# Two-layer decoder step on one core: the adaLN modulation computed tile by tile, most of it between other work

## What is computed

```python
for l in range(DEPTH):
    mod = (jax.nn.silu(c) @ p['w_ada'][l] + p['b_ada'][l])[:, None, :]
    shift1, scale1, gate1, shift2, scale2, gate2 = jnp.split(mod, 6, axis=-1)
    h = rmsnorm(x, p['g_mix'][l]) * (1 + scale1) + shift1
    mix, nb_a, nb_c, nb_d, v_n = token_mixers(h, buf_a[l], buf_c[l], buf_d[l], start_pos, l, p)
    x = x + gate1 * mix
    h = rmsnorm(x, p['g_ffn'][l]) * (1 + scale2) + shift2
    ...
    x = x + gate2 * f
```

## Time and profile before

| | |
|---|---|
| time, 3 runs | 1733.95, 1734.02, 1735.37 us (median 1734.02) |
| the profiled execution | 1732.69 us, its span from the first to the last instruction 1730.9 us |
| mean granted TensorE clock | 0.941 of full speed |
| busy: PE / PEld / DVE / ACT / POOL | 1488.1 / 1425.0 / 600.9 / 461.0 / 398.0 us |
| modulation's matmuls (L791), 768 | 104.0 us busy |
| modulation's rests on DVE (L1403), 48 | 110.0 us busy, 2293 ns each |
| modulation's rounding on ACT (L1157), 48 | 91.7 us busy, 1911 ns each |
| loads of `w_ada`, 48 of 1,024 KB | 11.2 us from issue to landing |

### The profile page before, as it was taken

The page is one execution under the profiler, slowest core; times in us unless marked ns, Lnnn a source line. Parts: engine busy times, 40 slices in busy tenths (PEclk is TensorE's granted clock), DMA queues, the critical chain, the costliest instruction groups (busy, mean ns, idle before and its releaser), DMA issues.

```text
span 1730.9 us, 26002 instructions
## 1 busy us (share of the span) xinstructions
PE 1488.1 (86%) x11320; PEld 1425.0 (82%) x11320; DVE 600.9 (35%) x815; ACT 461.0 (27%) x646; POOL 398.0 (23%) x288
## 2 busy tenths in 40 slices
PE   5777794797999999998968784999999986999992
PEld 4555694697999999997957682999999986999992
DVE  6757598734102111014696622011110110010115
ACT  6767421433222122222313312111111110010114
POOL 1101571253344333443450512000000000000005
PEclk9999897899999999998988897999999997999995
DMA  9999231113423323233221027589789792658644
GB/s 319 326 308 348 67 98 32 41 59 118 126 74 100 108 74 98 58 101 98 74 73 49 6 71 271 193 272 334 242 286 318 271 309 76 216 164 300 228 146 169
DMA packets 249973, 286.70 MB, mean 166 GB/s; under 512 B 7469, under 2 KB 241599, under 8 KB 249814
## 3 DMA queue, kind: packets, MB, share of 16 engines
q1 hardware_dynamic: 244886, 272.17, 48.4%
q0 software_dynamic: 3760, 12.09, 1.9%
q10 hardware_dynamic: 1200, 0.56, 0.1%
HBM read 266.45 MB, written 19.07 MB: 165 GB/s over the span
## 4 chain that ended last, share of the span: by engine, by line
PE 71%; DVE 15%; DMA 5%; issue 4%; SPq 2%; ACT 2%; POOL 1%; POOLq 0%; DVEq 0%; ACTq 0%
PE PP L746 29%; PE PP L1014 21%; PE PP L1026 11%; DVE work L1499 7%; DMA mem<-in_w_ada 4%; PE PP L759 2%; PE PP L791 2%; DVE stat L1595 2%; PE PP L720 1%; PE PP L731 1%; PE PP L985 1%; PE PP L996 1%; DVE stat L1428 1%; DVE mem L1441 1%; DVE mem_r L1437 1%
## 5 line engine op out<-in xcount | busy, mean ns | idle before, releaser
L746 PE MATMUL PP<-hT_r,mem_r 128*128 128x260 f32 x2624 | 428.5, 284 | 4.6 <-DVE xT L1453 3.2
L1014 PE MATMUL PP<-big,mem 128*128 128x144 f32 (+2 forms) x2816 | 372.9, 295 | 22.8 <-issue 22.0
L1014 PEld LDWEIGHTS PP<-big,mem 128*128 128x128 f32 x2816 | 370.7, 191 | 23.5 <-issue 22.4
L604 POOL TENSOR_TENSOR mem_r<-mem,mem_r 128x1024 fp32r<-128x1024 f32 (+1 forms) x108 | 279.0, 2598 | 407.7 <-ACT mem_r L1141 407.0
L746 PEld LDWEIGHTS PP<-hT_r,mem_r 128*128 128x128 f32 x2624 | 362.5, 189 | 6.5 <-issue 2.5
L746 PE MATMUL PP<-mem_r 128*128 128x260 f32 x1312 | 263.8, 283 | 0.0
L746 PEld LDWEIGHTS PP<-mem_r 128*128 128x128 f32 x1312 | 201.7, 188 | 0.0
L1026 PE MATMUL PP<-big,mem 128*128 128x144 f32 (+2 forms) x1408 | 193.5, 294 | 0.0
L1026 PEld LDWEIGHTS PP<-big,mem 128*128 128x128 f32 x1408 | 186.6, 190 | 0.0
L1689 DVE TENSOR_TENSOR big<-PP,stat 128x256 f32<-128x256 f32 x88 | 37.4, 425 | 394.4 <-ACT stat L1324 394.4
L702 POOL DMA_INDIRECT mem<-y_by_expert,place x10 | 9.9, 986 | 624.5 <-SPq L534 621.8
(11 more groups left out here) (236 smaller groups left out, 1100.5 us busy)
## 6 DMA issues: line engine op xcount, KB each, us to landing
mem<-in_w_moe SPq DMA_DIRECT2D x48, 1536.0 KB, 8.8
mem<-in_w_ada SPq DMA_DIRECT2D x48, 1024.0 KB, 11.2
mem<-in_w_moe SPq DMA_DIRECT2D x32, 1408.0 KB, 9.4
mem<-in_w_dense SPq DMA_DIRECT2D x20, 1024.0 KB, 5.5
mem<-in_w_in SPq DMA_DIRECT2D x16, 1024.0 KB, 5.4
mem<-in_w_moe SPq DMA_DIRECT2D x16, 1024.0 KB, 6.8
mem<-in_w_dense SPq DMA_DIRECT2D x16, 704.0 KB, 4.7
mem<-in_w_out SPq DMA_DIRECT2D x8, 1024.0 KB, 5.1
```

Source lines behind the costliest of these rows:

```text
L604: pool.tensor_tensor(r_(raw), raw, read_(hi), ALU.subtract).then_inc(w_lo, 1)
L746: mm = pe.matmul(PP[q][:, h, 0:HT], r_(w[:, k, :]), r_(x[:, k, HT * h:HT * h + HT]), start=(i == 0 and w is wh and x is hi), stop=(i == le ...
L1014: mm = pe.matmul(PP[w][:, f % 2, 0:n], raw[:, w, k, :], hn[:, k, 0:n], start=(k == 0), stop=(k == KD - 1))
```

## The change

The modulation of the first norm (16 tiles: shift1 and scale1 of layer 0) is computed up front in four pairs of chunks (`first_pair`), the other 80 tiles (`ADA`) later, in fills (`ada_fill`) at the places of `ADA_AT`. A tile is now a plain fp32 product with the weights stationary (128 x 128) and `c` moving: 9 columns, 8 matmuls a tile, straight into channel-major form. The rounding on ACT, the rests on DVE, the turning by transposes and POOL's part fall away; DVE adds the bias from PSUM (`mod_out`).

- Layer 0's mixer: 3 tiles after each of q = 4 to 11 (24). Layer 1's: 3 after each of q = 3 to 11 (27).
- Second norm of layer 0 and first norm of layer 1: 5 each, between the norm's sums and `two_products`.
- Dense part: 3 after each even f of the first half (18), 1 after f = 0 of the second.

Their weights come in tiles of 512 KB (rows of 128 channels, 512 bytes) into a ring of three in `adaw`; SP issues a tile's load when the tile three before it is done (`ada_loads`), queued between the other weights' loads. The results wait in the spare columns of PP3's second bank. SP now loads the tokens first, then pair 0, the small vectors, pair 1, the mixer's inputs; pairs 2 and 3 (pair 2 lies in `work`, the place of the squares) after the norm's sums.

```diff
-ADA_RING = 6
-NA = 24 // ADA_RING
+ADA_RING = 3
...
+ADA = [(0, j) for j in range(16, 48)] + [(1, j) for j in range(48)]
+IN_FILLS = [[(q, 3) for q in range(4, 12)], [(q, 3) for q in range(3, 12)]]
+FF_FILLS = [(0, f, 3) for f in range(0, 12, 2)] + [(1, 0, 1)]
+NORM_FILL = 5
+ADA_AT = {}
+_at = 0
+for _key, _n in ([(("in", 0, q), n) for q, n in IN_FILLS[0]] + [(("norm", 1), NORM_FILL)]
+                 + [(("ff", h, f), n) for h, f, n in FF_FILLS] + [(("norm", 2), NORM_FILL)]
+                 + [(("in", 1, q), n) for q, n in IN_FILLS[1]]):
+    ADA_AT[_key] = (_at, _at + _n)
+    _at += _n
+PAIRS_OUT = 4
+GROUPS = [("in", 0), ("norm", 1)] + [("ff", h, f) for h, f, _ in FF_FILLS] + [("norm", 2), ("in", 1)]
...
+        first_ada = [cut(mem, RING * SLOT, KD, 256), cut(mem, (RING + 1) * SLOT, KD, 256),
+                     cut(big, 5 * D + 4 * P + D, KD, 256), cut(big, 5 * D + 4 * P + D + SLOT, KD, 256),
+                     cut(wflat, 0, KD, 256), cut(wflat, SLOT, KD, 256),
+                     cut(mem, 2 * SLOT, KD, 256), cut(mem, 3 * SLOT, KD, 256)]
...
-            def ada_load(j, l, b):
-                sp.dma_start(ada_slot(j), w_ada_v[l][b]).then_inc(efull[j], 16)
+            def ada_loads(first, last):
+
+                for g in range(first, min(last, len(ADA))):
+                    l, j = ADA[g]
+                    if g >= ADA_RING:
+                        sp.wait_ge(ada_mm, 16 + g - ADA_RING + 1)
+                    sp.dma_start(adaw[:, g % ADA_RING], w_ada_v[l][j // 2][:, :, P * (j % 2):P * (j % 2) + P]).then_inc(ada_full[g % ADA_RING], 16)
+
+            def ada_after(*key):
+
+                first, last = ADA_AT[key]
+                ada_loads(first + ADA_RING, last + ADA_RING)
...
+            def first_pair(i):
+
+                for c, b in enumerate((4 + i, i)):
+                    sp.dma_start(first_ada[2 * i + c], w_ada_v[0][b]).then_inc(ada_in[i], 16)
...
+            for t in range(4):
+                sp.dma_start(xin[:, t, :], A["x_prompt"][0, P * t:P * t + P, :]).then_inc(x_in, 16)
+            sp.dma_start(xin[0:NS, 4, :], A["x_sample"].rearrange("b s d -> (b s) d")).then_inc(x_in, 16)
...
+            first_pair(0)
...
+            first_pair(1)
+            load(WIN0, chunk(WIN0))
+            mixer_loads(0)
+            sp.wait_ge(*norm_step(0, "sum", 1))
+            first_pair(2)
+            load(WIN0 + 1, chunk(WIN0 + 1))
+            first_pair(3)
+            ada_loads(0, ADA_RING)
+            for j in (2, 3):
+                sp.wait_ge(ada_mm, 12 + 2 * j - 2)
+                load(WIN0 + j, chunk(WIN0 + j))
             for n in range(WIN0, MOE - RING):
+                for l, base in ((0, WIN0), (1, WIN1)):
...
+            def ada_fill(*key):
+
+                for g in range(*ADA_AT[key]):
+                    first = min(a for k, (a, _) in ADA_AT.items() if k == key or (key[0] == "in" and k[:2] == key[:2]))
+                    at = HT + NQ * (g - first)
+                    pe.wait_ge(ada_full[g % ADA_RING], 16 * (g // ADA_RING + 1))
+                    for k in range(KD):
+                        mm = pe.matmul(PP[3][:, 1, at:at + NQ], adaw[:, g % ADA_RING, k, :], cs[:, k, :], start=(k == 0), stop=(k == KD - 1))
+                    mm.then_inc(ada_mm, 1)
+
+            def first_pair(i):
+
+                pe.wait_ge(ada_in[i], 32)
+                if i >= 2:
+                    pe.wait_ge(ada_out, i - 1)
+                for c in range(2):
+                    for m in range(2):
+                        at = NQ * (2 * c + m)
                         for k in range(KD):
-                            for lower, w in enumerate((ahi[:, j % 3], ada_slot(j))):
-                                mm = pe.matmul(PP[0][0:2 * NQ, j % 2, 0:256], r_(cs[:, k, :]), r_(w[:, k, :]),
-                                               start=(k == 0 and not lower), stop=(k == KD - 1 and bool(lower)))
+                            mm = pe.matmul(PP[1][:, i % 2, at:at + NQ], first_ada[2 * i + c][:, k, P * m:P * m + P], cs[:, k, :],
+                                           start=(k == 0), stop=(k == KD - 1))
                         mm.then_inc(ada_mm, 1)
-                        if j % 3 == 2:
-                            pe.wait_ge(ada_row, n + 3)
-                            for m in range(2):
-                                tr = pe.transpose(PP[1][:, 0, m * P:(m + 1) * P], modrow[:, m * P:(m + 1) * P], ident[:])
-                            tr.then_inc(ada_tr, 1)
...
+            first_pair(0)
+            pe.wait_ge(vec_in, 16 * NVEC)
+            for v in range(DEPTH):
+                tr = pe.transpose(PP[3][:, 0, v * NROWS:(v + 1) * NROWS], rows[0:NROWS, v, :], ident[0:NROWS, 0:NROWS])
+            tr.then_inc(pro_tr, 1)
+            pe.wait_ge(pro_dve, 8)
+            pe.wait_ge(const_dve, 1)
+            for j in range(KD):
+                norm_sum(0, j)
+            mixer_start(0)
+            for i in range(1, 4):
+                first_pair(i)
...
+                    pe.wait_ge(*ada_out_after("ff", 1, 0))
+                    ada_fill("norm", 2)
...
+                    if ("in", l, q) in ADA_AT:
+                        if l and q == 3:
+                            pe.wait_ge(*ada_out_after("norm", 2))
+                        ada_fill("in", l, q)
...
+                            if ("ff", h, f) in ADA_AT:
+                                if h == f == 0:
+                                    pe.wait_ge(*ada_out_after("norm", 1))
+                                if f:
+                                    pe.wait_ge(ff_free, FH * h + f)
+                                ada_fill("ff", h, f)
...
-                        dve.wait_ge(ada_hi, 24 * l + ADA_RING * i + j + 1)
-                        dve.tensor_tensor(r_(ada_slot(j)), ada_slot(j), read_(ahi[:, j % 3]), ALU.subtract).then_inc(ada_lo, 1)
...
+            def first_pair(i):
+
+                dve.wait_ge(ada_mm, 4 * i + 4)
+                src = PP[1][:, i % 2, 0:4 * NQ]
+                c = done(mod_out(src[:, 0:2 * NQ], 0, 8 * SCALE1 + 2 * i, 2))
+                mod_out(src[:, 2 * NQ:4 * NQ], 0, 8 * SHIFT1 + 2 * i, 2).then_inc(ada_out, 1)
+                dve.wait_ge(dchain, c)
+                dve.wait_ge(ada_out, i + 1)
+                link(scaled(0, SCALE1, "g_mix", 2 * i, 2))
+                dve.sem_inc(mods0, 1)
+
...
+                ada_group("in", l)
+                scaled(l, SCALE2, "g_ffn", 0, KD).then_inc(s["lnc_in"], 1)
...
```

More of the change, by code:

```diff
@@ L251, in trunk_program @@
         w_hi, w_lo = sem("w_hi"), sem("w_lo")
-        ada_hi, ada_lo = sem("ada_hi"), sem("ada_lo")
+        ada_in = [sem(f"first_ada_in{i}") for i in range(4)]
+        ada_full = [sem(f"ada_slot_full{i}") for i in range(ADA_RING)]
         g_hi, g_lo = sem("g_hi"), sem("g_lo")
@@ L471, in _ @@
                     mixer_loads(1)
+                for l, base in ((0, WIN0), (1, WIN1)):
+                    if base <= n < base + 6 and ("in", l, 2 * (n - base) + 1) in ADA_AT:
+                        ada_after("in", l, 2 * (n - base) + 1)
+                if n == WOUT0 + 3:
+                    ada_after("norm", 1)
+                h, c = divmod(n - DENSE, PER_H)
+                if n >= DENSE and c % 2 == 1 and ("ff", h, c - 1) in ADA_AT:
+                    ada_after("ff", h, c - 1)
+                if n == WIN1 - 1:
+                    ada_after("norm", 2)
             sp.wait_ge(*step(1, "po_done", KD))
@@ L778, in _ @@
             pe.transpose(PP[2][:, 1, 0:96], rows[0:96, 2, :], ident[0:96, 0:96]).then_inc(pro_tr, 1)
-            pe.wait_ge(pro_dve, 1)
-            pe.sem_inc(ada_mm, 3)
-            for l in range(DEPTH):
-                with pe.Fori(0, NA) as i:
-                    for j in range(ADA_RING):
-                        n = 24 * l + ADA_RING * i + j
-                        pe.wait_ge(ada_lo, n + 1)
-                        pe.wait_ge(ada_row, n + 1)
+            def ada_fill(*key):
[6 more added lines that the diff above has]
+                    mm.then_inc(ada_mm, 1)
@@ L821, in _, with mixer_start @@
-            for l in range(DEPTH):
+            def mixer_start(l):
                 pe.wait_ge(*step(l, "mx_in", 16 * 16))
@@ L918, in _ @@
                 if l == 0:
+                    pe.wait_ge(*ada_out_after("in", 0))
+                    ada_fill("norm", 1)
                     for h in range(2):
@@ L1191, in norm_act @@
                 root(2, stat[:], D, ns["root"])
-                for j in (KD - 2, KD - 1) if tag else range(UNIT_SLOTS):
-                    upper(u + j)
+                if tag:
+                    for j in (KD - 2, KD - 1):
+                        upper(u + j)
+                else:
+                    act.wait_ge(ada_mm, 4)
                 for j in range(KD):
+                    if tag == 0:
+                        act.wait_ge(mods0, j // 2 + 1)
+                        if j >= 4:
+                            upper(j - 4)
                     act.wait_ge(*norm_step(tag, "xhat", j + 1))
```

(35 more changed lines are left out.)

186 lines of the change are left out of this document (60 added, 126 removed).

## The result

| | before | after |
|---|---|---|
| time, median | 1733.99 us, 4 runs (1733.48 to 1735.37) | 1821.38 us, 4 runs (1817.86 to 1823.57) |
| span of the profiled execution | 1730.9 us | 1816.1 us |
| mean granted clock | 0.941 | 0.892 |
| busy PE / PEld / DVE / ACT / POOL | 1488.1 / 1425.0 / 600.9 / 461.0 / 398.0 | 1665.0 / 1631.1 / 460.8 / 347.3 / 419.3 |

A forecast was written before the change was run, and what follows sets the result against it. PE bounds the chain (fp32r products, experts), after a load-bound first stage. Prologue -99, mixers (20.3 + 32) and (25.6 + 36), dense part (33.4 + 24), norms 10: +82, 1816 us; range 1668 to 1855.

The forecast's parts named there:

- A tile costs 1.76 us, set by the weight load: Each tile on PE: 16 weight loads 0.11 us apart at 2.4 GHz, 1.76 us; 3.5 us at 1.2 GHz.
- rival 3: A tile costs 0.4 us, the issue gap as bound and weight loads hidden: 1609 us; chance 0.02.
- The prologue gains 99: Start to `two_products` done: 103.9 us against 202.9 at half clock, a gain of 99; 127 at full clock.
- the term of the pairs: Prologue, first norm's tiles at half clock: pair 0 takes 14.1 us, pairs 1 to 3 take 42.2.
- Room under the taps and the sum of the mixers: Mixers: 21.9 us of waiting each hides tiles; 20.3 and 25.6 us paid, plus 32 and 36 for the clock.
- 4 us for each fill's clock: Fills of three: clock falls in or just behind each; 3.7 us computed, 4 taken; 32, 36 and 24 in all.
- Norms, 5 each: Layer 0's second and layer 1's first norm: five tiles at a falling clock cost 5 us each; 0 at full clock.
- Loads and SP cost nothing: Tile loads and SP's queue, all fills: costed at nothing; the dense part's term is 33.4 us of tiles and 24 of clock.
- Rival 4: Late tiles, some 2 us a fill: the forecast and 46 us more, 1862 us; chance 0.03.
- The experts: 0: Router to the end: forecast to change by 0 us.
- one comparison of two stretches of 4 and 6 us: Old trace: clock fell at 94.1 us after narrow matmuls (90 to 94), but stayed 1.00 with 256-column ones (36 to 42).
- rival 1: Clock holds in all fills and pairs because PE never stands still: 1681 us (1665 to 1700); chance 0.29.

The follow-up runs named there:

- wide_five: The changed kernel with the nine columns repeated 5 times (45 columns) in the 23 fills only, the prologue's pairs left narrow: 1759.5 us.
- wide_sp: The changed kernel with 117 columns in every tile's matmuls and layer 1's 19 mixer loads issued 14 weight chunks later: 1696.86 us, ratio 0.9782.
- sp_half: The changed kernel with layer 1's 19 mixer loads issued 14 weight chunks later on SP, in the dense part's second half: 1809.55 us, ratio 1.0432.
- sp_late: The changed kernel with layer 1's 19 mixer loads issued four weight chunks later on SP: 1820.31 us, ratio 1.0491.
- wide_all: The changed kernel with the nine columns repeated 13 times (117 columns) in every tile's matmuls, fills and pairs: 1709.11 us, ratio 0.986.

## Why the prediction was right

The forecast was +82 and the two spans differ by 85.2. The range, 1668 to 1855, took in a held clock as well as a fallen one, so that the time lies in it says little; what the prediction is worth is in its steps:

- *A tile costs 1.76 us, set by the weight load.* Right: 1.85 us for a tile alone; with 117 columns 5.51 for three, and 19 in 33.5; pairs at 0.216 us a record at half clock. That 9, 45 and 117 columns take nearly the same at full clock is what speaks for the load. The Trainium skill ("TensorE: Matmul & The Clock Gate", LDWEIGHTS (loading the stationary operand)) gives P / 1.2 ns for a load of P columns, 107 ns for 128; the trace of wide_five has 5.45 us / 48 = 114 ns at full clock, 7% above. The 25 ns a record of rival 3 are far from it.
- *The prologue gains 99.* 106.8: the term of the pairs was too large, by 3.6 in pair 0 and 5.2 in pairs 1 to 3, since pairs 0 and 1 began at full clock; that was in the text for fills and left out here. So the first product came at 82.6 us, outside the 85 to 93 that the text gave as its sign. (Rows 3 and 8 give 15.0 and 14.9 us for `two_products`, where the text has 14.8 and 14.7.)
- *Room under the taps and the sum of the mixers.* +49.2 and +57.4 for +52.3 and +61.6. With the clock held (wide_sp) the stretch is 91.9, where the text gave 93.
- *4 us for each fill's clock.* (122.3 - 91.9) / 8 = 3.8, (143.0 - 109.7) / 9 = 3.7, and in the dense part without its late tile (434.7 - 413.1) / 6 = 3.6. The computed 3.7 was the better number than the 4 taken above it. The clock of 0.65 named for q = 4 to 11 doesn't follow from either: 32 us lost in 111 give 0.71, and 0.73 was measured.
- *Norms, 5 each.* +3.9 and +4.7; with the clock held they cost nothing, as the text had it.
- *Loads and SP cost nothing.* Wrong in one place, and by the text's own sign (PE waits for `ada_slot_full`): +70.4 in the dense part is 13.0 above the term. The late tile is all of it: without it (sp_half) the dense part is +55.1, 2.3 below the term. The step that failed is "SP's waits for `ada_mm` stand behind loads already issued": it looked at what the tiles' waits hold up, and not at what holds up the tiles, the 19 issues that stood in the very trace of before. Rival 4 had late tiles as 2 us in every fill; it is 10.4 us of waiting in one.
- *The experts: 0.* +5.5 in the profiled execution, and from the router on wide_sp, sp_late and sp_half are 8 to 13 us longer than in the old kernel, with the same work. PE's waits put down to "issue" there are 22.0 us in two before and 23.4 to 27.3 in six or seven in these, which explains a part. The rest stays open.

What came out below the forecast, in the early pairs (-7.8) and in the mixers and norms (-8.7), and what came out above it, in the dense part and the experts (+18.5), nearly cancel: that the total is 3 us off, closer than its terms, is luck.

The sign hung on one comparison of two stretches of 4 and 6 us, and the runs bear it out: same weights, same loads, 9 columns or 117, 112 us. The comparison itself was thin. The clock of the old kernel fell also in the midst of wide matmuls (L791, 256 columns) where PE had stood still between them, here from 138.62 to 140.54:

```profile
140.00:142.00 2.00, 1.33 (x10) 0.97 (x11) 1.88 (x1) 1.43 (x4) 0.25 (x1) 0.98 1.11 349
142.00:144.00 2.00, 2.00 (x11) 1.39 (x10) 1.05 (x2) 1.33 (x1) 0.99 (x4) 0.50 1.10 348
```

So the fall at 94.1 us, with 1.2 us of idle time ahead of it, could not tell narrow matmuls from idle time; wide_all did. The sign was right on weak evidence, which the chance of 0.29 for rival 1 said.

Rival 1's mechanism (PE never stands still, and that is enough) is what is excluded; its time is what a kernel gets that widens the operand (1696.9 in wide_sp, against 1681; most of the rest is 6 us more prologue, half of it PE's wait of 3.0 for the mixer's inputs, and the experts' 8). The Trainium skill (same page, HAM oscillation) tells of a clock that falls in idle gaps between matmuls. The earlier trace rows agree with that: 0.55 in 268 to 270, with PE idle. But here it also fell, to a mean of 0.73, with PE busy for 111.00 of 111.00 us, and stayed at 0.50 for 24.00 of 24.00; of that the section says nothing.

## What to carry to other kernels

A matmul with few moving columns and new weights costs its weight load (here 0.11 us at full clock for 9, 45 or 117 columns), and a run of them costs the clock as well, for itself and for the wide work behind it. Repeating the operand's columns by a stride of 0 was nearly free up to 117 columns and kept the clock there; with 45 it fell at three fills of eight. Split narrow work into short bursts (here single tiles of 1.85 us kept the clock) or widen it. And when a small load is put on a queue between others, list what is issued ahead of it at each place, not only what it holds up; a wait in a trace is free room only if the engine isn't reading registers in it.
